# Second block's mixers: stacked rounded parts for the attention scores, memory's projection moved ahead of the input projection, preparation steps placed between its chunks, and another order of the state's heads

## What is computed

```
h    = rms_norm(x, mix_norm_g);  proj = h @ w_in            # 17 tiles of 128 columns
qa (6 heads of 64), ka, va (2 heads), pb (10 tiles), qm (4 heads) = split(proj)
qa, ka = rms_norm per head;  out_a = sliding_window_attention(qa, ka, va, sinks, rel_bias)
pb   = pb + mu * (previous token's pb - pb)                 # token shift
out_b = rwkv7_mixer(pb, ...)                                # a state per head, 6 heads of 64
mk, mv = split(rms_norm(mem, mem_norm_g) @ w_mem_kv)        # 4 tiles of 128 columns
mk, qm = rms_norm per head;  out_m = memory_attention(qm, mk, mv)
x    = x + concat(out_a, out_b, out_m) @ w_out;   x = x + conv_ffn_2(rms_norm(x))
```

## Time and profile before

| what | us |
|---|---|
| runs: median of 3 (lowest, highest) | 2742.24 (2740.48, 2742.33) |
| the profiled execution's own time | 2742.9 |
| its span, first to last instruction | 2740.8 |
| PE busy / DVE / ACT / POOL | 2424.6 / 1319.9 / 918.4 / 731.4 |
| second block's projections, 1744 to 1868 | 124 |
| preparation, 1868 to 1887 | 19 |
| second attention, 1887 to 2005 | 118 |
| token shift to the first product behind it | 18 |
| rest of the state mixer, to 2310 | 287 |

### The profile page before, as it was taken

One profiled execution on the slowest core, in us unless ns is written; L12 is line 12 of the kernel. 1 busy time (PEld: TensorE's weight loads), 2 busy tenths in 40 slices (PEclk: granted clock), 3 DMA queues, 4 the chain that ended last, 5 costly groups with the idle time before them and its releaser, 6 DMA issues.

```text
span 2740.8 us, 35407 instructions
## 1 busy us (share of the span) xinstructions
PE 2424.6 (88%) x13423; PEld 1956.3 (71%) x13423; DVE 1319.9 (48%) x2197; ACT 918.4 (34%) x1385; POOL 731.4 (27%) x344
## 2 busy tenths in 40 slices
PE   4888557999999997999799999998956998999998
PEld 3777346888888885777677877784425887778877
DVE  3699954333123335488433133554455453542351
ACT  4211045432123214355354144423332122442341
POOL 2122111232222222200234444341002221344442
PEclk8999778999999998999899999997567888999999
DMA  7666201222122212100233333332000000233332
GB/s 242 215 194 214 88 23 39 62 61 69 55 61 67 63 55 66 54 1 1 62 99 97 88 92 98 96 92 58 1 0 1 1 1 23 85 90 94 91 98 88
DMA packets 337220, 204.68 MB, mean 75 GB/s; under 512 B 5917, under 2 KB 335303, under 8 KB 336967
## 3 DMA queue, kind: packets, MB, share of 16 engines
q1 hardware_dynamic: 331915, 194.02, 23.7%
q10 hardware_dynamic: 5180, 8.94, 1.0%
HBM read 200.74 MB, written 2.20 MB: 74 GB/s over the span
## 4 chain that ended last, share of the span: by engine, by line
PE 39%; issue 31%; DVE 14%; POOL 11%; ACT 2%; DVEq 1%; DMA 1%; ACTq 0%; POOLq 0%
POOL w_lo L501 10%; PE ps L559 9%; PE ps L560 9%; PE ps L561 9%; DVE ps L1200 8%; PE ps L1465 2%; PE ps L2344 1%; PE ps L1493 1%; PE ps L2342 1%; PE ps L2334 1%; PE ps L1480 1%; DVE n_t L945 1%; PE ps L760 1%; DVEq L2520 0%; DVE inv L2518 0%
## 5 line engine op out<-in xcount | busy, mean ns | idle before, releaser
L501 POOL TENSOR_TENSOR w_lo<-raw,w_hi 128x1024 fp32r<-128x1024 f32 (+1 forms) x253 | 644.9, 2551 | 1514.2 <-ACT w_hi L531 1496.2
L559 PE MATMUL ps<-x_hi,w_hi 128*128 128x512 f32 (+1 forms) x1864 | 680.0, 365 | 72.1 <-DVE x_lo L1103 49.7
L560 PE MATMUL ps<-x_lo,w_hi 128*128 128x512 f32 (+1 forms) x1864 | 669.0, 359 | 0.0
L561 PE MATMUL ps<-x_hi,w_lo 128*128 128x512 f32 (+1 forms) x1864 | 667.6, 358 | 0.0
L531 ACT ACTIVATE w_hi<-raw 128x1024 fp32r<-128x1024 f32 (+1 forms) x251 | 280.9, 1120 | 841.2 <-PE ps L561 837.5
L559 PEld LDWEIGHTS ps<-x_hi,w_hi 128*128 128x128 f32 x1864 | 356.7, 191 | 144.7 <-issue 67.6
L560 PEld LDWEIGHTS ps<-x_lo,w_hi 128*128 128x128 f32 x1864 | 357.2, 192 | 52.1 <-issue 2.6
L561 PEld LDWEIGHTS ps<-x_hi,w_lo 128*128 128x128 f32 x1864 | 356.7, 191 | 51.5
L1367 DVE SCALAR_TENSOR_TENSOR f_a<-ps,prm,f_a 128x511 f32<-128x511 f32 (+2 forms) x176 | 116.1, 681 | 375.5 <-ACT f_b L1333 363.8
L559 PE MATMUL ps<-g_hi,w_hi 128*128 128x512 f32 (+1 forms) x704 | 259.0, 368 | 14.7 <-DVE g_lo L1376 10.4
L560 PE MATMUL ps<-g_lo,w_hi 128*128 128x512 f32 (+1 forms) x704 | 257.1, 365 | 0.0
(11 more groups left out here) (320 smaller groups left out, 3114.8 us busy)
## 6 DMA issues: line engine op xcount, KB each, us to landing
raw<-in_ffn_w_up SPq DMA_DIRECT2D x88, 512.0 KB, 3.9
ada_tail<-in_ada_w SPq DMA_DIRECT2D x22, 1024.0 KB, 8.4
raw<-in_ffn_w_down SPq DMA_DIRECT2D x32, 704.0 KB, 4.5
raw<-in_w_up SPq DMA_DIRECT2D x44, 512.0 KB, 3.9
ada_s<-in_ada_w SPq DMA_DIRECT2D x20, 1024.0 KB, 8.7
raw<-in_conv_w_pw SPq DMA_DIRECT2D x24, 512.0 KB, 4.1
raw<-in_w_down SPq DMA_DIRECT2D x16, 704.0 KB, 4.6
raw<-in_w_in SPq DMA_DIRECT2D x17, 512.0 KB, 4.0
```

The lines of the kernel that those rows point to most:

```text
L501: pool.tensor_tensor(M.w_lo[:, slot, 0:K * P], M.raw[:, slot, 0:K * P], M.w_hi[:, slot, 0:K * P].bitcast(F32), ALU.subtract).then_inc(lo_r ...
L559: pe.matmul(o, wh, hi[:, k, t0:t0 + tn], start=(k == 0), stop=False)
L560: pe.matmul(o, wh, lo[:, k, t0:t0 + tn], start=False, stop=False)
L561: return pe.matmul(o, wl, hi[:, k, t0:t0 + tn], start=False, stop=(k == K - 1))
```

## The change

1. `STREAMS`: `mem_kv` now comes before `w_in`. MEMO's parts are made ahead of MIX's. PE starts with memory's column sum and its four chunks, then `first_two` and the other chunks of `w_in`. Chunks of `w_in` are taken in the order 0, 1, 2, 3, 15, 16, 4, 5 ... 14.
2. The preparation is gone as a stage: its steps and the eight head norms (one per chunk, behind chunks 1 to 8; a query's product goes to PSUM, where `q_high` on ACT and `q_low` on DVE cut it into parts, two 64-row instructions each) stand between the chunks. PE's fp32 products there: memory's keys doubled behind chunk 8 (4 of 256 columns), the bias rows behind 10 (1 of 384), keys doubled behind 11 (2 of 512) with 4 transposes, 4 transposes behind 12, the bias behind 14 (3 of 512). Behind chunk 16 DVE makes the bias's rest (`blo`, 3 of 512 columns). The final norm's product moves from chunks 13 to 16 into `w_out_dve`.
3. Token shift: for the ten chunks of `pb`, DVE scales in PSUM, ACT writes (1-mu) times it, DVE adds mu times the token before. `rw_pre_dve` has no shift any more.
4. Scores: a query head is stored as 128 rows, its rounded part above or below its rest; keys, doubled over both halves, are stored as rounded part and rest. Two fp32r products per head replace one fp32 product over 64 rows; the bias takes two fp32r products instead of an fp32 one. The sink becomes one more column of the scores, from a 2-column product, and its exponential, minimum and sum go away.
5. `x0`, `state`, `y`: two heads (rows 0 to 63 and 64 to 127) take turns inside each kind of product.

```diff
-STREAMS += [("w_in", 17, 8), ("mem_kv", 4, 8), ("w_out", 8, 8)]
+STREAMS += [("mem_kv", 4, 8), ("w_in", 17, 8), ("w_out", 8, 8)]
+W_IN_ORDER = [0, 1, 2, 3, 15, 16, 4] + list(range(5, 15))
+SHIFTED_AT = 7
...
         if stream == "down11" and m:
+            parts_dve(dve, MEMO, m - 1)
             parts_dve(dve, MIX, m - 1)
-            parts_dve(dve, MEMO, m - 1)
...
+    def memo_stats_pe(pe):
+        pe.wait_ge(MEMO.sum, done(7))
+        pe.wait_ge(evac, done(Q0["mem_kv"] - 1))
+        pe.matmul(memo_ps(), ones, M.n_t[:, 0, SEQ:TOK], start=True, stop=True).then_inc(mix_stat, 1)
...
+    def w_in_pe(pe):
+        memo_stats_pe(pe)
+        pe.wait_ge(MEMO.x, done(KD))
+        for u in range(4):
+            products(pe, "mem_kv", 0, u, MEM)
+        first_two(pe, "w_in", LAT, MIX, lambda: mix_stats_pe(pe))
+        for p in range(1, 17):
+            if p >= 2:
+                products(pe, "w_in", p // 4, p % 4, LAT)
+            if p - 1 < 8:
+                head_sum(pe, p - 1)
...
     def w_in_act(act):
+        memo_stats_act(act)
         for u in range(4):
+            high(act, "mem_kv", 0, u)
+        mix_stats_act(act)
+        for p in range(17):
+            high(act, "w_in", p // 4, p % 4)
+            if p >= SHIFTED_AT:
+                V_S.after(act, f"y{p}")
+                S_S.mark(act.activation(M.pj[:, c, :], M.pair((Q0["w_in"] + p) % 4, 0, SEQ), ACT.Identity,
+                                        scale=M.omu[:, c - 5:c - 4], bias=0.0), f"os{p}")
+            if 1 <= p <= 8:
+                head_rms(act, p - 1)
+            if p < 8:
+                head_square(act, p)
...
     def w_in_dve(dve):
+        for p in range(17):
+            dve.wait_ge(tile_done, done(q0 + p + 1))
+            if p < SHIFTED_AT:
+                dve.tensor_tensor(M.pj[:, W_IN_ORDER[p], :], o, M.rt0[:, :], ALU.mult).then_inc(evac, 1)
+            else:
+                V_S.mark(dve.tensor_tensor(o, o, M.rt0[:, :], ALU.mult), f"y{p}")
+            if p > SHIFTED_AT:
+                add_previous(p - 1)
+            if 1 <= p <= 8:
+                head_norm(dve, p - 1)
+            if 4 <= p <= 6:
+                q_low(dve, p - 4)
+            if 8 <= p <= 9:
+                q_low(dve, p - 4)
...
+        add_previous(16)
...
-                scores = [(0, nb, M.pj[half:half + HD, hh // 2, i * P:(i + 1) * P],
-                           M.qg[half:half + HD, g, lo * P:(i + 1) * P], True),
-                          (0, nb, ident, M.bias[:, hh, 2 * P - nb:2 * P], False)]
+                scores = [(0, nb, q, M.k2_hi[:, g, lo * P:(i + 1) * P], True),
+                          (0, nb, q, M.k2_lo[g][:, lo * P:(i + 1) * P], False),
+                          (0, nb, M.fr2[:, 0:P], M.bias[:, hh, 2 * P - nb:2 * P], False),
+                          (0, nb, M.fr2[:, 0:P], M.bias_lo[:, hh, 2 * P - nb:2 * P], False),
+                          (nb, 2, M.fr2[:, P:2 * P], M.sk2[:, hh, :], True)]
...
+                heads.append(Unit([(0, CTX, q, M.x_hi[:, hh, SEQ:TOK], True), (0, CTX, q, M.x_lo[:, hh, SEQ:TOK], False)],
...
-        for i in range(10):
-            x, d = M.pj[:, 5 + i, :], M.dd[:, i % 2, :]
-            dve.tensor_tensor(d[:, 1:SEQ], x[:, 0:SEQ - 1], x[:, 1:SEQ], ALU.subtract)
...
-            for hh in H6:
-                mm = pe.matmul(by_parity(hh), M.m4[:, n % 2, hh, 2 * P:3 * P], M.tok[:, 2, hh * HD:(hh + 1) * HD],
-                               start=True, stop=(n == 0))
-                if n:
+            for c in C3:
+                for hh in (2 * c, 2 * c + 1):
+                    mm = pe.matmul(by_parity(hh), M.m4[:, n % 2, hh, 2 * P:3 * P], M.tok[:, 2, hh * HD:(hh + 1) * HD],
+                                   start=True, stop=(n == 0))
+                for hh in (2 * c, 2 * c + 1) if n else ():
                     mm = pe.matmul(by_parity(hh), kk_t[c][r, t], M.z[r, c, :], start=False, stop=True)
...
             if st == "mixers":
-                mix_prep_pe(pe)
-                S_S.after(pe, "bias")
+                pe.wait_ge(evac, done(Q0["w_out"]))
+                S_S.after(pe, "mv")
+                V_S.after(pe, "blo")
                 att_pe(pe, ATT2)
```

More of the change, by code:

```diff
@@ L476, in one @@
                          w_src[name][:, :, bass.ds(c, P)]).then_inc(s_raw[slot], 16)
-        if full >= 2 and name != "qkv":
+        if full >= 2 and name not in ("qkv", "w_in"):
             with sp.Fori(0, full) as it:
@@ L1407, in build_in, with __init__ @@
     class Unit:
-        def __init__(self, scores, nk, sink, neg_sink, parts, place):
-            self.scores, self.nk, self.sink, self.neg_sink = scores, nk, sink, neg_sink
+        def __init__(self, scores, nk, parts, place):
+            self.scores, self.nk = scores, nk
             self.parts, self.place = parts, place
@@ L1574, in exps @@
                            bias=M.sm_neg[:, b:b + 1], accum_out=M.sm_sum[:, b:b + 1])
-            if x.sink is not None:
-                act.activation(M.sm_sink[:, b:b + 1], x.sink, ACT.Exp, bias=M.sm_neg[:, b:b + 1])
             act.drain().then_inc(att_p, 1)
@@ L1839, in vector_steps @@
         return out_
[L1842 removed]
+    T_S = Steps("step_t", [f"head{i}" for i in (6, 7, 0, 1, 2, 3, 4, 5)] + ["mkd", "rr", "kd", "vt", "mv", "bias"]
                 + [f"z{n}" for n in N4] + [f"a{c}" for c in C3] + ["kk0", "bonus0"] + [f"g{c}" for c in C3]
@@ L1952, in w_in_pe @@
-    def w_in_pe(pe):
-        first_two(pe, "w_in", LAT, MIX, lambda: mix_stats_pe(pe))
-        for it, u in peeled_chunks(pe, 17):
-            peeled = isinstance(it, int)
-            if not (peeled and 4 * it + u < 2):
-                products(pe, "w_in", it, u, LAT)
-            if peeled and 4 * it + u in (2, 3):
-                head_sum(pe, u - 2)
-                if u == 3:
-                    head_sum(pe, 2)
-                    head_sum(pe, 3)
-        for u in range(4):
-            V_S.after(pe, f"head{max(u + 2, 3)}")
-            products(pe, "mem_kv", 0, u, MEM)
-            if u < 2:
-                head_sum(pe, 4 + u)
@@ new lines, in build_in, with head_tile, head_square @@
+    HEADS = [6, 7, 0, 1, 2, 3, 4, 5]
+    def head_tile(i):
+        if i < 4:
+            return M.pj[:, i, :], SEQ, "attn_k_norm_2" if i == 3 else "attn_q_norm_2", (2, 3, 0, 1)[i]
+        if i < 6:
+            return M.pj[:, 11 + i, :], SEQ, "mem_q_norm_2", i - 2
+        return M.mkv[:, i - 6, :], CTX, "mem_k_norm_2", i - 6
+    def head_square(act, j):
+        i = HEADS[j]
+        x, w, _, _ = head_tile(i)
+        act.wait_ge(evac, done(Q0["w_in"] + i + 1 if i < 6 else Q0["mem_kv"] + i - 5))
+        if j >= 2:
+            T_S.after(act, f"head{HEADS[j - 2]}")
+        S_S.mark(act.activation(M.n_sq[:, j % 2, 0:w], x, ACT.Square), f"sq{i}")
@@ new lines, in head_sum, with head_rms @@
+    def head_sum(pe, j):
+        i = HEADS[j]
+        _, w, _, r = head_tile(i)
+        S_S.after(pe, f"sq{i}")
+        if i < 2:
+            pe.wait_ge(mix_sd, done(3))
+        elif i < 6:
+            V_S.after(pe, ("head6", "head7", "qlo0", "qlo1")[i - 2])
+        T_S.mark(pe.matmul(odd(r, w), head1, M.n_sq[:, j % 2, 0:w], start=True, stop=True), f"head{i}")
+    def head_rms(act, j):
+        i = HEADS[j]
+        _, w, _, r = head_tile(i)
+        T_S.after(act, f"head{i}")
+        if j >= 2:
+            V_S.after(act, f"head{HEADS[j - 2]}")
+        S_S.mark(act.activation(M.n_t[:, j % 2, 0:w], odd(r, w), ACT.Sqrt, scale=1.0 / HD, bias=eps_col), f"rms{i}")
@@ new lines, in w_in_dve, with add_previous @@
+        memo_stats_dve(dve)
+        for u in range(4):
+            dve.wait_ge(tile_done, done(Q0["mem_kv"] + u + 1))
+            dve.tensor_tensor(M.mkv[:, u, :], M.pair((Q0["mem_kv"] + u) % 4, SEQ, TOK), M.rm[:, :], ALU.mult)\
+                .then_inc(evac, 1)
+        mix_stats_dve(dve)
+        def add_previous(p):
+            c = W_IN_ORDER[p]
+            S_S.after(dve, f"os{p}")
+            dve.scalar_tensor_tensor(out=M.pj[:, c, 1:SEQ], in0=M.pair((q0 + p) % 4, 0, SEQ - 1),
+                                     scalar=M.col("rwkv_mu_2", c - 5), in1=M.pj[:, c, 1:SEQ], op0=ALU.mult, op1=ALU.add)\
+                .then_inc(evac, 1)
```

422 lines of the change are left out of this document (223 added, 199 removed), and 2 rows, old and new, of the table h_count.

## The result

The changed kernel takes 2652.38 us (median of 4, 2651.79 to 2653.69) against 2741.83 us of the kernel before on the same chip: ratio 0.9675, interval [0.9658, 0.9692]. I had forecast 2676 and a range of 2656 to 2706, from the median of 2742.24 that the kernel before had in its first three runs. The sign was right. The gain is 89.5 us where I had 66.7, and the time lies outside the range. The direction of one part was wrong: I had the way to the attention's first maximum 1.5 us longer, and it became 2.7 shorter.

What follows compares the result with a forecast made beforehand. PE was taken to bound the long projection, and the second attention at 1.2 GHz nearly throughout. Terms: +1.5 to the first score, -43 attention, -15.7 shift, -9.5 heads, summing to -66.7, about 2676 us; range 2656 to 2706.

Steps and rivals of the forecast that it cites:

- to the first maximum: Start, projection and preparation up to the second attention's first maximum: together 1.5 us longer.
- Memory first, and the start: Start of the second block's projection: PE waits for DVE's memory sums, `w_in` chunk 2 comes late, +23.4 us.
- Between the chunks: Projection behind chunk 2: chunks keep 5.44 us, added fp32 PE work costs +9.8 us, DVE hides.
- rival D: Projection: DVE does not keep up between the chunks and the start comes late, +12, 2688 us; chance 0.08.
- Second attention: Second attention: cheaper scores and a partly higher clock bring 118 us to 75, -43.
- the first units of 128 keys ... and half of the next 18 at the low level: Second attention's front: six units at 1.3 us and nine at 2.36 at the low clock, the rest at full clock.
- rival B: Second attention: full clock from the first units on, -52 in place of -43, 2667 us; chance 0.15.
- Rival A: Second attention: clock stays low, -24 in place of -43, 2695 us; chance 0.22.
- Shift: Token shift behind the second attention: its 15.8 us leave the path, -15.7 us.
- Heads: State mixer's `x0` and `y`: two heads together change rows half as often and can overlap, -9.5 us.
- the first theory: Second attention: the kind of product, fp32 or fp32r, decides TensorE's clock; fp32 scores would give about 2703 us.

Runs made afterwards that it cites:

- before_rows128: Kernel before, with only the second attention's query-key products taking all 128 rows instead of a head's 64: 2693.07 us against 2741.24.
- f32r_rows64: Changed kernel with each second-attention unit's two query-key products cut to 64 rows, still fp32r, query's small part left out: 2685.78 us.
- warm_gap: Changed kernel with seventeen fp32r products of 512 columns put in PE's pause between the last chunk and the first score: 2653.01 us.
- heads_in_before: Kernel before with only the new order of heads in x0, state and y: 2723.42 us against 2740.6, ratio 0.994.

## Why the prediction was wrong

**The sum.** The parts missed by 4.2 us (to the first maximum), 11.4 (attention) and 8.2 (heads), all on the same side; none of these alone leaves the range.

**Memory first, and the start** (+23.4 forecast, +19.9 measured). Right in its mechanism: PE stood 6.85 us for DVE's sums and chunk 2 came late. Of the 3.5 us, 2.2 were there when PE began (1749.82 for 1752; 1.4 of them because the projection before ended at 1742.97, not 1744.4), 0.8 more at memory's third chunk (1758.39 for 1761.4) and 0.5 by `w_in`'s chunk 2. The weight stream kept the pace that I gave it. Two slips in this term are under 1 us: 1778 and 1.7 make 1779.7, and of the 6.7 us between the last sum and chunk 2 in the kernel before, 6.9 cannot remain.

**Between the chunks** (+9.8 forecast). 1782.62 to the last tile product's end at 1883.93 - 3.89 = 1880.04 is 97.4 us; I had 97.9. DVE hid as argued, and rival D's late DVE did not happen. The tail to the first score was 3.9, forecast 4.4. The 19.9, 9.3 and 3.9 us added here are together less than the 36.1 removed, so this half gained 2.7 us by the first maximum instead of losing 1.5.

**Second attention** (-43 forecast, -54.4 measured). The units at full clock were right: sixteenth unit to first memory unit 13.5 us for nine, forecast 13.5; memory's first maximum to its sixteenth 21.6 for fifteen units, forecast 21.8. The last unit and the end behind it took 6.8 us (1939.82 to 1946.61), where I had 1.45 and 9. The failed step is "the first units of 128 keys ... and half of the next 18 at the low level": 29.0 us for fifteen units, measured 19.5. The clock rose at 1896, after ten units, before the first product with the values; the units with values that I had priced at 2.7 each never met the low level. The 256-key units that did meet it, still without values, started 1.2 to 1.4 us apart, where I had 1.66. Behind the step stands a wrong reason: I compared the mix with the first attention's and took fp32r for what decides. before_rows128 and the pairs with 64 rows show that it was the 64-row products, by their rows or by the changes that they bring; the 64-row query products of the earlier trace rows in the trace of the kernel before, against the first attention's 128-row ones of the earlier trace rows, could have raised that question. That reading would have pointed to rival B, 2667 with a chance of 0.15; B's full clock from the first unit did not come either. Rival A (2695) would have needed the clock to stay low: f32r_rows64 was at 0.50 throughout both windows, at 2685.8.

The rule of the Trainium skill, "TensorE: Matmul & The Clock Gate", HAM oscillation, that pauses between bursts bring the clock down, does not order these runs: PE was busy 22.00 of 22 us at 0.50 and 17.03 of 22 at 1.00. At the seam ahead of the attention the trace agrees: behind the pause of 3.89 us the clock was 0.50, and with the pause filled, in warm_gap, 1.00.

**Shift** (-15.7 forecast, -15.8 measured). Right.

**Heads** (-9.5 forecast, between -4 and -11; -17.7 in the stage, -17.2 by heads_in_before). The products' own price was nearly right: a pair in `x0` takes 0.96 us (below, of the changed kernel), forecast 0.95, and a whole `y` 4.56, forecast 4.14. The term was mis-sized because I priced only the calls themselves. They gave 12.4 us, where I took 9.5; the clock of the steps between them rose too, which the untouched groups show, and the other 4.9 lie there. No bound of mine let a faster stage raise its neighbours' clock.

```profile
2096.80 0.66 PE L2471 MATMUL ps<-tok,m 128*128 128x64 f32 x4
2097.39 0.44 PE L2475 MATMUL ps<-z,pj 64*128 64x64 f32 x4
2097.76 0.66 PE L2471 MATMUL ps<-tok,m 128*128 128x64 f32 x4
```

**The range.** The misses of the attention and of the heads have one sign, and the clock is the main cause of the first and an unpriced part of the second. I had put the two as independent, and the range's lower end did not hold both.

## What to carry to other kernels

Where TensorE is busy all the time and still at 0.50, look at how many rows its products fill, and how often that number changes, before counting instructions. Here stacking a head's two parts gave back the clock of all but the attention's first 11 us, and letting two 64-row products of different rows overlap raised the state mixer's mean clock from 0.80 to 0.89. A gain that raises the clock is larger than the lengths of the edited instructions, so price it over the stage. Test such a reason by changing one property alone (the rows, then the type): here the first theory fell at its first run, and the rows and the changes between them are still to be separated.

## What the runs showed of the hardware that was not expected

- Rows and clock, same columns, same instruction counts: from 1896 to 1940 fp32 over 64 rows 0.50, over 128 rows 1.00 (48 us of the whole), fp32r likewise (33 us). Why is not shown; only that it was so in three pairs of kernels. In the units of 128 keys the clock was 0.50 with 128 rows as well.
- Seventeen products of 512 columns in a pause of 3.9 us kept the clock up in it and changed nothing of the time.
- At the low level, putting a 128-row product behind a 64-row one costs some 0.3 us: in f32r_rows64 two starts on from the last 64-row product it is 0.72 us later (1921.83 to 1922.55), in the changed kernel, with the same columns and 128 rows throughout, 0.43 (1891.42 to 1891.85).

```profile
1921.83 0.41 PE L1500 MATMUL ps<-k_lo,pj_r 64*128 64x256 f32 x1
1922.17 0.58 PE L1500 MATMUL ps<-bias,fr 128*128 128x256 f32 x1
1922.55 0.41 PE L1500 MATMUL ps<-bias_lo,fr 128*128 128x256 f32 x1
```

```profile
1891.42 0.41 PE L1500 MATMUL ps<-k_lo,pj_r 128*128 128x256 f32 x1
1891.63 0.41 PE L1500 MATMUL ps<-bias,fr 128*128 128x256 f32 x1
1891.85 0.41 PE L1500 MATMUL ps<-bias_lo,fr 128*128 128x256 f32 x1
```
